# A transformer block in split fp32: seven pairs of the third layer by seven products, and tokens put in order by GpSimd

## The chip, the cores and the metric

The kernel runs on one core of one Trainium2 chip. The metric is the device time of one execution in microseconds (us). Before the change the median of three runs is 1440.94 us (1440.66 to 1441.42).

## The reference

One encoder block on x (512 tokens, width 1024, float32): a half-step SwiGLU feed-forward (the first layer here), a mixer of dilated attention and a gated recurrence (the second), and another half-step feed-forward (the third).

```python
def rmsnorm(x, g):
    return x * lax.rsqrt(jnp.mean(x * x, axis=-1, keepdims=True) + EPS) * g

def swiglu(x, w_in, w_out):
    gate, up = jnp.split(x @ w_in, 2, axis=-1)
    return (jax.nn.silu(gate) * up) @ w_out

h = rmsnorm(x, ffn1_pre_norm);  x = x + 0.5 * rmsnorm(swiglu(h, w_ffn1_in, w_ffn1_out), ffn1_post_norm)
h = rmsnorm(x, mix_pre_norm)
z = h @ w_in            # q, k, v of 3 head groups (dilations 1, 4, 16), 5 HGRN parts, 2 gates
y = (sigmoid(gA) * (attention @ P_A) + sigmoid(gH) * (hgrn2 @ P_H)) @ w_out
x = x + rmsnorm(y, mix_post_norm)
h = rmsnorm(x, ffn2_pre_norm);  x = x + 0.5 * rmsnorm(swiglu(h, w_ffn2_in, w_ffn2_out), ffn2_post_norm)
```

w_ffn2_in is 1024 x 5632 and w_ffn2_out 2816 x 1024.

## The kernel before

Activations lie transposed: 128 features to a tile, 512 tokens along the row; xt holds x in 8 such tiles (KT). Every large product is made in three passes of TensorE in a rounded fp32 format (F32R): a factor is split into a high part (rounded) and a low part (the rest), and high x high, high x low and low x high are summed in PSUM (product, project). hh and hl are the high and low parts of the normalised tokens, whi and wlo those of a weight block.

Weights come in blocks of 128x1024 floats. SyncE loads a block into raw (load_block); ScalarE copies it to whi (head), VectorE subtracts to get wlo (tail), TensorE multiplies (project). head(pair, s) and tail(pair, s) prepare the next pair's block. The counters are raw_in, head_done, split_done and block_done. Each engine runs its own list in the order in which the code writes it; only counters tie the lists together.

First half of a feed-forward: 22 pairs, each a gate block (s = 0) and an up block (s = 1) for 128 of the 2816 columns. VectorE scales each result by rstd (gated, up), ScalarE takes Silu (gate), VectorE multiplies (glu) into a_raw, which is split into ah and al for the second half.

In the first layer pairs 6 to 21 are done as Strassen products. The two column blocks, two halves of the features and two halves of the tokens give a 2x2 block product, done in 7 instead of 8 quarter products of 256 tokens (strassen_in_pe, with the order Q_ORDER and banks BANKS). VectorE forms the weight sums c and d, ScalarE and VectorE split a, b, c and d into high and low (a_part, b_part, c_part, d_part, sum_part), and results are seeded and joined through PSUM (seed_c11, u2_out, u4_out, c22_joined, c21_joined). The tokens are normalised beforehand with a negative gain (normed), and their sums formed and split once (token_sums_early and _late, b_tail, t_tail).

In the third layer (ffn3_in_pe, ffn_in_act, ffn_in_dve) all 22 pairs are direct: 0 and 1 by token halves, pair 2 into banks 5 and 6, the others in turn into banks 0 and 1 (ffn_in_turn, ffn_in_loop). After pairs 4 and 5 TensorE transposes x (turn_x, 4 tiles each time), ScalarE copies it to x_tok (leave_x) and GpSimd stores it to DRAM, from where the last stage takes it back. The second half of the layer uses Strassen sums over pairs of a_raw tiles from pair 6 on; six of its eight sets are formed during the first half (pair_sums, pair_head, pair_low), one after every two pairs.

In the mixer the values of the three head groups come first (v_pe). There the tokens are the stationary operand (128 tokens to an output bank) and the weights move. Group 0 takes tokens in order, in two halves, each tile as soon as VectorE has it (counter pre2 "ready"; VectorE's chain for a tile ends in the operation on line 1557). Groups 1 and 2 take the tokens by their remainder modulo 4, for the dilations: every fourth column of hh and hl is read as the stationary operand (line 2098). Between groups 1 and 2 the tokens are normalised anew into hh and hl (h_norm, h_head, h_low). GpSimd stores a table of bias vectors and loads the bias tiles of the head pairs; in the recurrence it copies one tile a head.

Of the kernel before, what the change touches and what calls it, by code (L numbers as in the profile page):

```python
# [19 lines left out]
ALU = mybir.AluOpType  # L20
ACT = mybir.ActivationFunctionType
AXIS_X = mybir.AxisListType.X
F32 = mybir.dt.float32
# [12 lines left out]
R = 4  # L36
# [41 lines left out]
AFTER_IH_S_SUM, AFTER_IH_T_SUM = IN_S_SUM + 8, IN_T_SUM + 4  # L78
IH_0 = 2 * FIRST["ih"]
# [38 lines left out]
def build(nc, wstream, x_t, params, last_gain, rel_bias, onehot, consts, out):  # L118
    with ExitStack() as ctx:
# [44 lines left out]
        ones = ones_r[:].bitcast(F32)  # L164
        cst = place("cst", [P, 2 * P + 2 * S])
# [80 lines left out]

        at[0] = arena + 4 * S * (2 * FT + 1)
# [112 lines left out]

        at[0] = arena
# [615 lines left out]
        def ffn3_in_pe(pe):  # L977
# [30 lines left out]
            ffn_in_turn(pe, 3, 4)  # L1008
# [15 lines left out]
        def pair_sums(dve, m):  # L1024
# [4 lines left out]
            if m < 2:  # L1029
                dve.wait_ge(sem("x_turned"), KT)  # L1030
            elif m < AHEAD_KP:
                dve.wait_ge(sem("pool_stored"), 16 * (1 + TT))
            else:
                dve.wait_ge(block_done, LAST)
# [40 lines left out]
        def ffn_in_loop(pe, n, j0):  # L1075
            with pe.Fori(j0, FT) as j:
                ffn_in_turn(pe, n, j)

        def ffn_in_act(act, n):
            first = FIRST[f"ffn{n}_in"]  # L1080

            def gate(j):
                act.wait_ge(sem("gated"), GATED_BEFORE[n] + j + 1)
                act.wait_ge(sem("glu"), BEFORE[n] + j + 1)
                nc.scalar.activation(silu[:], tmp[:, 0, :], ACT.Silu).then_inc(sem("silu"), 1)

            def pair(m):
                j = N_PLAIN + 2 * m
                for k in (j, j + 1):
                    turn(k, False)  # L1090
                if m < AHEAD_KP:
                    pair_head(act, m)

            def a_head(j):
                act.wait_ge(sem("glu"), BEFORE[n] + j + 2)
                nc.scalar.activation(ah[:, bass.ds(j, 1), :].rearrange("p a n -> p (a n)"), tmp[:, 1, :],
                                     ACT.Copy).then_inc(sem("a_head"), 1)

            def turn(j, whole=True):
                head(act, first + j, 0)  # L1100
                gate(j)
                head(act, first + j, 1)
                if whole:
                    a_head(j)
# [6 lines left out]
            a_head(0)  # L1111
            gate(1)
            head(act, first + 2, 1)
            a_head(1)
            gate(2)
            a_head(2)
            for j in range(3, 5):
                turn(j)
            leave_x(act, 0)
            turn(5)  # L1120
            leave_x(act, 1)
            for m in range(N_KP):
                pair(m)
# [2433 lines left out]
```

## Time and profile before

| what | value |
|---|---|
| median of 3 runs | 1440.94 us |
| profiled execution | 1441.15 us, span 1439.0 us, mean granted clock 0.999 |
| busy TensorE matmul / weight loads | 1431.7 / 1227.9 us |
| busy VectorE / ScalarE / GpSimd | 903.7 / 669.4 / 23.3 us |
| values, groups 1 and 2 | from 377 to 424 us |
| third layer, pairs 7 to 21 of the first half | from about 1161 us |

In the profile PE is TensorE's matmuls, PEld its weight loads, DVE VectorE, ACT ScalarE, POOL GpSimd, SP SyncE. Matmuls are pipelined: the next starts before one ends, so what one costs is read from the distance of starts and not from its length. An output is written ps<-b,w with the moving operand and the stationary one. ps is PSUM.

### The profile page before, as it was taken

The numbers are of one execution on the slowest core, as the hardware profiler recorded it, in microseconds if no ns is written. First come the engines' busy times: TensorE is split into PE (matmuls) and PEld (weight loads), VectorE is DVE, ScalarE is ACT, GpSimd is POOL, SyncE is SP. The second block draws the span as 40 slices with busy tenths as digits, with TensorE's granted clock in tenths as the row PEclk, the third lists the DMA queues.
The fourth block names the chain that finished last, engine by engine and source line by source line (L and its number), as shares of the span: only waits on it lengthen the run. The fifth ranks groups of instructions, "written<-read, shape, count | busy, mean of one in ns | idle before, by whom it ended". The sixth has DMA issues, their size and how long they took to land.

```text
span 1439.0 us, 21208 instructions
## 1 busy us (share of the span) xinstructions
PE 1431.7 (99%) x8104; PEld 1227.9 (85%) x8104; DVE 903.7 (63%) x1424; ACT 669.4 (47%) x1083; POOL 23.3 (2%) x43
## 2 busy tenths in 40 slices
PE   9999999999999999999999999999999999999998
PEld 8899999888898888888888888888889888888886
DVE  7888875335753455567866766664548555564975
ACT  5455555334532546555446554553445333233542
POOL 0000000000100000000000000000000000000000
PEclk9999999999999999999999999999999999999999
DMA  5333223324333323225322122224331243324653
GB/s 198 118 118 114 93 89 118 132 90 130 96 110 89 92 74 89 63 74 169 115 97 74 59 87 63 69 72 129 106 103 45 88 148 101 97 92 143 218 182 130
DMA packets 44317, 153.71 MB, mean 107 GB/s; under 512 B 5287, under 2 KB 5287, under 8 KB 44240
## 3 DMA queue, kind: packets, MB, share of 16 engines
q1 hardware_dynamic: 41472, 143.67, 31.3%
q0 software_dynamic: 2624, 8.95, 2.0%
q8 instruction: 51, 0.84, 0.2%
q14 instruction: 26, 0.21, 0.0%
q10 hardware_dynamic: 144, 0.04, 0.0%
HBM read 147.63 MB, written 4.23 MB: 106 GB/s over the span
## 4 chain that ended last, share of the span: by engine, by line
PE 98%; ACT 1%; DVE 1%; issue 0%; DVEq 0%; ACTq 0%
PE ps L470 21%; PE ps L471 21%; PE ps L472 21%; PE ps L637 4%; PE ps L638 4%; PE ps L639 4%; PE ps L1701 3%; PE ps L1700 3%; PE ps L1702 3%; PE ps L2530 1%; PE ps L2100 1%; PE ps L2101 1%; PE ps L2102 1%; PE ps L2913 1%; PE ps L2510 1%; PE ps L2933 1%
## 5 line engine op out<-in xcount | busy, mean ns | idle before, releaser
L470 PE MATMUL ps<-hh,whi 128*128 128x512 f32 x960 | 379.2, 395 | 0.1
L472 PE MATMUL ps<-hh,wlo 128*128 128x512 f32 x960 | 374.0, 390 | 0.0
L471 PE MATMUL ps<-hl,whi 128*128 128x512 f32 x960 | 373.9, 389 | 0.0
L416 DVE TENSOR_TENSOR wlo<-raw,whi 128x1024 fp32r<-128x1024 f32 x172 | 210.5, 1224 | 250.4 <-ACT whi L411 250.3
L411 ACT ACTIVATE whi<-raw 128x1024 fp32r<-128x1024 f32 x172 | 181.8, 1057 | 380.9 <-PE ps L472 356.3
L470 PEld LDWEIGHTS ps<-hh,whi 128*128 128x128 f32 x960 | 180.1, 188 | 42.6 <-issue 3.2
L472 PEld LDWEIGHTS ps<-hh,wlo 128*128 128x128 f32 x960 | 180.2, 188 | 38.1
L471 PEld LDWEIGHTS ps<-hl,whi 128*128 128x128 f32 x960 | 180.3, 188 | 35.7
L470 PE MATMUL ps<-ah,whi 128*128 128x512 f32 (+1 forms) x192 | 71.5, 372 | 0.0
L472 PE MATMUL ps<-ah,wlo 128*128 128x512 f32 (+1 forms) x192 | 71.3, 371 | 0.0
L471 PE MATMUL ps<-al,whi 128*128 128x512 f32 (+1 forms) x192 | 71.3, 371 | 0.0
L1700 PE MATMUL ps<-whi,ah 128*128 128x512 f32 x112 | 43.6, 389 | 0.0
L1702 PE MATMUL ps<-whi,al 128*128 128x512 f32 x112 | 43.6, 389 | 0.0
L1701 PE MATMUL ps<-wlo,ah 128*128 128x512 f32 x112 | 43.6, 389 | 0.0
L470 PEld LDWEIGHTS ps<-ah,whi 128*128 128x128 f32 x192 | 36.2, 188 | 6.3
L471 PEld LDWEIGHTS ps<-al,whi 128*128 128x128 f32 x192 | 36.2, 188 | 6.3
L472 PEld LDWEIGHTS ps<-ah,wlo 128*128 128x128 f32 x192 | 36.2, 188 | 6.2
L1145 DVE TENSOR_TENSOR tmp<-ps,rstd 128x512 f32<-128x512 f32 x22 | 15.2, 690 | 41.7 <-PE ps L472 41.6
L1134 DVE TENSOR_TENSOR tmp<-ps,rstd 128x512 f32<-128x512 f32 x22 | 15.2, 690 | 34.5 <-PE ps L472 32.0
L2594 ACT ACTIVATE prob_t<-ps 128x512 f32<-128x512 f32 x32 | 17.4, 595 | 40.2 <-PE ps L2530 38.6
L1675 ACT ACTIVATE whi<-ring 128x1024 fp32r<-128x1024 f32 x20 | 21.1, 1062 | 27.6 <-PE ps L1702 27.6
L2586 ACT ACTIVATE prob<-prob,neg_max 128x256 f32<-128x256 f32 x64 | 31.6, 503 | 2.8 <-DVE neg_max L2702 2.5
(576 smaller groups left out, 3007.4 us busy)
## 6 DMA issues: line engine op xcount, KB each, us to landing
raw<-in_wstream SPq DMA_DIRECT2D x189, 512.0 KB, 3.5
w_raw<-in_wstream SPq DMA_DIRECT2D x32, 512.0 KB, 4.3
ring<-in_wstream SPq DMA_DIRECT2D x20, 512.0 KB, 4.3
xt<-in_x_t SPq DMA_DIRECT2D x16, 256.0 KB, 4.3
raw_early<-in_wstream SPq DMA_DIRECT2D x8, 512.0 KB, 4.4
raw_late<-in_wstream SPq DMA_DIRECT2D x4, 512.0 KB, 3.9
x_dram<-x_tok POOLq DMA_DIRECT2D x4, 512.0 KB, 4.1
x_tok<-x_dram POOLq DMA_DIRECT2D x4, 512.0 KB, 5.8
```

The lines of the kernel that those rows point to most:

```text
L411: nc.scalar.activation(whi[:, s, :], raw[:, s, :], ACT.Copy).then_inc(head_done, 1)
L416: nc.vector.tensor_tensor(wlo[:, s, :], raw[:, s, :], whi[:, s, :].bitcast(F32), ALU.subtract).then_inc(split_done, 1)
L470: nc.tensor.matmul(out, w, m, start=start, stop=False)
L471: nc.tensor.matmul(out, w, ml, start=False, stop=False)
L472: return nc.tensor.matmul(out, wl, m, start=False, stop=stop)
L637: nc.tensor.matmul(out, w, b, start=q in (1, 7) and k == 0, stop=False, skip_group_check=True)
L638: nc.tensor.matmul(out, w, b_l, start=False, stop=False, skip_group_check=True)
L639: last = nc.tensor.matmul(out, wl, b, start=False, stop=k == KT // 2 - 1, skip_group_check=True)
L1700: nc.tensor.matmul(out, a, w, start=start, stop=False, skip_group_check=True)
L1701: nc.tensor.matmul(out, a, wl, start=False, stop=False, skip_group_check=True)
L1702: return nc.tensor.matmul(out, a_low, w, start=False, stop=stop, skip_group_check=True)
L2586: nc.scalar.activation(prob[:, e, lay, :], prob[:, e, lay, :], ACT.Exp, bias=stat(neg_max, n, lay, e), scale=-1.0, accum_out=stat(row_sum, ...
```

## The change

Two parts.

In the third layer pairs 7 to 13 become Strassen products, with the same steps and order as in the first layer. VectorE normalises the tokens into b3_raw and forms four token sums (the first layer keeps three); ScalarE and VectorE split them to b3_high, b3_low, t3_high, t3_low. The weights of even steps lie in the place of hh and hl, so pair 14 reads b3_high and b3_low, and during it the tokens are copied back to hh and hl (h_back). From pair 14 on the results need no scaling by rstd: ScalarE takes Silu straight from PSUM (gate_plain) and VectorE multiplies straight from PSUM (glu_plain). ah and al of tiles 0 to 5 are made three at a time in pairs 14 and 15, and the six early sets for the second half in pairs 14 to 20. turn_x(0) comes ahead of pair 4 and turn_x(1) ahead of pair 5; x goes to x_early, in two halves, each stored by itself. Pairs 5 and 6 use banks 2, 3 and 0, 1.

In the values GpSimd copies hh and hl of each tile into hp_high and hp_low with the tokens ordered by remainder, groups 1 and 2 read these, the new tokens of group 2 are written in that order, and GpSimd copies them back to hh and hl before attention. Two counters of the constant tables become one.

```diff
@@ ffn3_in_pe @@
-            ffn_in_turn(pe, 3, 4)
             pe.wait_ge(sem("gated"), GATED_BEFORE[3] + 3)
             pe.wait_ge(sem("up"), GATED_BEFORE[3] + 3)
             turn_x(pe, 0)
-            ffn_in_turn(pe, 3, 5)
+            ffn_in_turn(pe, 3, 4)
             pe.wait_ge(sem("x_left"), 4)
             turn_x(pe, 1)
-            ffn_in_loop(pe, 3, 6)
+            pe.wait_ge(sem("gated"), GATED_BEFORE[3] + 2)
+            project(pe, first + 5, 0, ps[:, 2, :], hh, hl)
...
+            strassen3_pe(pe)
+            for j in range(J4, FT):
+                early = j == J4
+                pe.wait_ge(sem("silu"), BEFORE[3] + (j if early else j + 1))
+                if j == J4 + 1:
+                    pe.wait_ge(sem("h_high"), S3_H + KT + 4)
+                    pe.wait_ge(sem("h_low"), S3_H + KT + 4)
+                h, h_l = (b3_high, b3_low) if early else (hh, hl)
+                project(pe, first + j, 0, ps[:, 0, :], h, h_l)
...
+        Q3_ORDER = []
+        for _j in range(J3, J4):
+            Q3_ORDER += [(1, _j), (7, _j)]
+            if _j > J3:
+                Q3_ORDER.append((3, _j - 1))
+            Q3_ORDER.append((6, _j))
+            if _j > J3:
+                Q3_ORDER.append((4, _j - 1))
+            Q3_ORDER += [(2, _j), (5, _j)] if _j < J4 - 1 else [(5, _j), (2, _j)]
+        Q3_ORDER += [(3, J4 - 1), (4, J4 - 1)]
...
@@ VectorE, pair 14 on @@
+            for j in range(J4, FT):
+                tail(dve, first + j, 0)
+                if j < J4 + 2:
+                    a_lows(3 * (j - J4), 3 * (j - J4) + 3)
+                if j > J4 and j - J4 - 1 < AHEAD_KP:
+                    for part in range(2):
+                        pair_low(dve, j - J4 - 1, part)
+                glu_plain(j)
+                if j - J4 < AHEAD_KP:
+                    pair_sums(dve, j - J4)
+                tail(dve, first + j, 1)
...
@@ v_pe @@
-                        if t == 0 and g == 2:
-                            pe.wait_ge(sem("h_low"), IN_H + kt + 1)
+                        if t == 0:
+                            pe.wait_ge(*((sem("h_turned"), KT + kt + 1) if g == 1 else (sem("h_low"), IN_H + kt + 1)))
...
-                        m = [x[:, kt, :].rearrange("p (u r) -> p r u", r=R)[:, t, :] for x in (hh, hl)]
+                        m = hp_high[kt][:, t, :], hp_low[kt][:, t, :]
...
@@ gpsimd @@
+            for kt in range(KT):
+                pool.wait_ge(*counted("pre2", "ready", KT + kt + 1))
+                nc.gpsimd.tensor_copy(hp_high[kt][:], hh[:, kt, :].rearrange(by_rest, r=R)).then_inc(sem("h_turned"), 1)
+            pool.wait_ge(block_done, 2 * FIRST["v"] + 2)
+            for kt in range(KT):
+                nc.gpsimd.tensor_copy(hp_low[kt][:], hl[:, kt, :].rearrange(by_rest, r=R)).then_inc(sem("h_turned"), 1)
             pool.wait_ge(sem("vec_out"), 2)
...
+                        pool.wait_ge(sem("h_turned"), 2 * KT)
+                        for d in range(KT):
+                            pool.wait_ge(sem("h_low"), IN_H + d + 1)
+                            for x, turned in ((hh, hp_high[d]), (hl, hp_low[d])):
+                                nc.gpsimd.tensor_copy(x[:, d, :].rearrange(by_rest, r=R), turned[:]
+                                                      ).then_inc(sem("h_turned"), 1)
```

GpSimd's list from the constant tables to the bias tiles, before; vec_dram is the table of bias vectors.

```order
L3299 DMA hot_sb<-in_onehot 33x1024
L3300 DMA cst<-in_consts 128x1280
L3302 DMA vec_dram<-vec_sb 8x1024 [waits vec_out]
L3320 DMA bias_156<-vec_dram 128x384 [waits post_x,pool_stored]
L3321 DMA bias_156<-vec_dram 128x2x128
...
L3311 DMA v_mid<-v_tok 64x1536 [waits v_scaled]
```

The same place after; the lines with "..." between them are seven more copies of the same kind each time.

```order
L3737 DMA cst<-in_consts 128x1280
L3740 COPY hp_high_242<-hh 128x512 [waits pre_ready]
...
L3743 COPY hp_low_250<-hl 128x512 [waits block_done]
...
L3745 DMA vec_dram<-vec_sb 8x1024 [waits vec_out]
L3768 DMA bias_179<-vec_dram 128x384 [waits post_x,pool_stored]
L3769 DMA bias_179<-vec_dram 128x2x128
...
L3756 COPY hh<-hp_high_242 128x4x128 [waits h_low,h_turned]
L3756 COPY hl<-hp_low_250 128x4x128
...
L3759 DMA v_mid<-v_tok 64x1536 [waits v_scaled]
```

Sixteen copies stand ahead of the bias table's DMA, and sixteen ahead of v_mid's.

VectorE's list in the third layer for one direct pair and the sums behind it, before (a pair's gate, up and product, the weights' low parts between them).

```order
L1134 TENSOR_TENSOR tmp<-ps,rstd 128x512 [waits silu,block_done]
L416 TENSOR_TENSOR wlo<-raw,whi 128x1024 [waits head_done]
L1145 TENSOR_TENSOR tmp<-ps,rstd 128x512 [waits glu,block_done]
L416 TENSOR_TENSOR wlo<-raw,whi 128x1024 [waits head_done]
L1150 TENSOR_TENSOR a_raw<-silu,tmp 128x512 [waits up,silu]
L1036 TENSOR_TENSOR t_raw_a<-a_raw 128x256 [waits glu,x_turned]
```

One Strassen step of the third layer after, from one join to the next.

```order
L1546 TENSOR_TENSOR tmp<-ps,tmp 128x256 [waits glu,q_left]
L1506 TENSOR_TENSOR w_even_c_raw<-w_raw 128x1024 [waits block_done,raw_in1,raw_in0]
L1534 TENSOR_TENSOR w_even_a_low<-w_raw,w_even_a_high 128x1024 [waits head_done]
L1524 TENSOR_TENSOR w_even_d_raw<-w_even_c_raw,w_raw 128x512 [waits s_sum]
L1514 TENSOR_TENSOR w_even_c_low<-w_even_c_raw,w_even_c_high 128x1024 [waits s_sum,s_head]
L1528 TENSOR_TENSOR w_even_d_raw<-w_even_d_raw,w_raw 128x512 [waits s_sum]
L1551 TENSOR_TENSOR tmp<-ps,y_67 128x256 [waits block_done]
L1435 TENSOR_TENSOR a_raw<-silu,tmp 128x512 [waits q_joined,silu]
L1514 TENSOR_TENSOR w_even_d_low<-w_even_d_raw,w_even_d_high 128x1024 [waits s_sum,s_head]
L1540 TENSOR_TENSOR w_even_b_low<-w_raw,w_even_b_high 128x512 [waits head_done]
```

A pair's five operations become ten, in which the scaling by rstd no longer occurs.

## Rows read from the trace of the kernel before

**Rows 1.** The page, busy time and chain that ended last.

```profile
PE 1431.7 (99%) x8104; PEld 1227.9 (85%) x8104; DVE 903.7 (63%) x1424; ACT 669.4 (47%) x1083; POOL 23.3 (2%) x43
...
PE 98%; ACT 1%; DVE 1%; issue 0%; DVEq 0%; ACTq 0%
```

**Rows 2.** Waits of TensorE (us in total, times, longest).

```profile
PE ps L3343 <- DVE eps L3394: 1.7, 1, 1.7
```

**Rows 3.** Timeline (start, length us) and one stretch by engine, first and third layer.

```profile
99.75 0.28 PE L637 MATMUL ps<-b_high,w_even_a_high 128*128 128x256 f32 x1
...
199.68 0.28 PE L637 MATMUL ps<-b_high,w_even_a_high 128*128 128x256 f32 x1
...
99.75:199.68 99.93, 99.93 (x843) 99.93 (x841) 80.65 (x101) 53.28 (x80) 0.00 (x0) 1.00 0.31 106
...
1157.34 0.39 PE L470 MATMUL ps<-hh,whi 128*128 128x512 f32 x1
...
1195.42 0.39 PE L470 MATMUL ps<-hh,whi 128*128 128x512 f32 x1
```

**Rows 4.** The page's costliest groups, VectorE.

```profile
L416 DVE TENSOR_TENSOR wlo<-raw,whi 128x1024 fp32r<-128x1024 f32 x172 | 210.5, 1224 | 250.4 <-ACT whi L411 250.3
...
L1145 DVE TENSOR_TENSOR tmp<-ps,rstd 128x512 f32<-128x512 f32 x22 | 15.2, 690 | 41.7 <-PE ps L472 41.6
```

**Rows 5.** Timeline of TensorE, first Strassen pair of the first layer.

```profile
77.97 0.28 PE L639 MATMUL ps<-b_high,w_first_a_low 128*128 128x256 f32 x1
78.23 0.38 PE L637 MATMUL ps<-b_high,w_first_c_high 128*128 128x256 f32 x1
78.45 0.28 PE L638 MATMUL ps<-b_low,w_first_c_high 128*128 128x256 f32 x1
```

**Rows 6.** Timeline of TensorE, third layer, ahead of pair 4.

```profile
1124.60 0.39 PE L472 MATMUL ps<-hh,wlo 128*128 128x512 f32 x1
1125.12 0.47 PE L470 MATMUL ps<-hh,whi 128*128 128x512 f32 x1
1125.43 0.40 PE L471 MATMUL ps<-hl,whi 128*128 128x512 f32 x1
```

**Rows 7.** Two lines (ns min/median/max) and TensorE's timeline, values' last groups.

```profile
L2100 PEld LDWEIGHTS ps<-whi,hh x64: 307/309/314, 376.9 to 423.2; 128*128 128x128 f32 x64
...
L2278 PEld LDWEIGHTS ps<-whi,hl x24: 187/188/188, 676.0 to 713.4; 128*128 128x128 f32 x24
...
376.93 0.63 PE L2100 MATMUL ps<-whi,hh 128*128 128x512 f32 x1
...
394.78 0.91 PE L2115 MATMUL ps<-cst,rstd 32*128 32x32 f32 x8
395.62 0.62 PE L2100 MATMUL ps<-whi,hh 128*128 128x512 f32 x1
...
424.12 0.40 PE L470 MATMUL ps<-hh,whi 128*128 128x512 f32 x1
```

**Rows 8.** Timeline of VectorE and TensorE, values' first group.

```profile
363.74 0.48 DVE L1557 SCALAR_TENSOR_TENSOR hl<-xt,par,hh 128x256 fp32r<-128x256 f32 x1
...
364.76 0.40 PE L2079 MATMUL ps<-whi_v,hh 128*128 128x512 f32 x1
...
371.68 0.48 DVE L1557 SCALAR_TENSOR_TENSOR hl<-xt,par,hh 128x256 fp32r<-128x256 f32 x1 [0.18 <-ACT hh L1463]
...
375.58 0.39 PE L2081 MATMUL ps<-wlo_u,hh 128*128 128x512 f32 x1
```

**Rows 9.** GpSimd's copy (a line, the timeline) and the last new tokens' split.

```profile
L3327 POOL COPY y<-ih_tok x8: 606/615/616, 721.1 to 934.2; 128x512 f32 x8
...
721.15 0.61 POOL L3327 COPY y<-ih_tok 128x512 f32 x1 [180.02 <-DVE ih_tok L2358]
...
721.47 0.48 DVE L3034 MEMSET rstd<- 128x512 f32 x1
...
405.43 1.35 DVE L2186 TENSOR_TENSOR hl<-tmp,hh 128x512 fp32r<-128x512 f32 x2
```

More of the change, by code:

```diff
@@ new lines, in glu_plain, with a_lows @@
+            def glu_plain(j):
+                dve.wait_ge(block_done, 2 * (first + j) + 2)
+                dve.wait_ge(sem("silu"), BEFORE[3] + j + 2)
+                if j == J4:
+                    dve.wait_ge(sem("h_low"), S3_H + KT + 4)
+                nc.vector.scalar_tensor_tensor(out=a_raw[:, j, :], in0=ps[:, 1, :], scalar=-1.0, in1=silu[:], op0=ALU.mult,
+                                               op1=ALU.mult).then_inc(sem("glu"), 1)
+            def a_lows(j0, j1):
+                flat = "p k n -> p (k n)"
+                dve.wait_ge(sem("a_head"), BEFORE[3] + j1)
+                high, low, whole = [x[:, j0:j1, :].rearrange(flat) for x in (ah, al, a_raw)]
+                nc.vector.tensor_tensor(low, whole, high.bitcast(F32), ALU.subtract).then_inc(sem("a_tail"), j1 - j0)
@@ L1191, in ffn_in_dve @@
             tail(dve, first + 2, 0)
[L1192 removed]
+            glu_whole(0)
             gated(1, 2)
             up(1, 3)
[L1195 to L1196 removed]
+            normed(0)
+            glu_whole(1)
             gated(2, 5)
             up(2, 6)
[L1199 to L1203 removed]
+            tail(dve, first + 2, 1)
+            glu_whole(2)
@@ new lines, in ffn3_in_dve @@
+            for kt in (4, 1, 5):
+                normed(kt)
+            gated(3, 0)
+            tail(dve, first + 3, 0)
+            for kt in (2, 6, 3, 7):
+                normed(kt)
+            up(3, 1)
+            tail(dve, first + 3, 1)
+            glu_whole(3)
+            token_sums_early()
+            gated(4, 0)
+            tail(dve, first + 4, 0)
+            token_sums_late()
+            b_tail(0)
+            up(4, 1)
+            tail(dve, first + 4, 1)
+            glu_whole(4)
@@ new lines, in ffn3_in_dve @@
+            b_tail(1)
+            for k in range(KT // 2):
+                t_tail(k)
+            gated(5, 2)
+            tail(dve, first + 5, 0)
+            b_tail(2)
+            b_tail(3)
+            c_sum(J3)
+            tail(dve, first + 5, 1)
+            up(5, 3)
+            glu_whole(5)
+            gated(6, 0)
+            a_part(J3)
+            d_sums(J3)
+            up(6, 1)
+            glu_whole(6)
+            for j in range(J3, J4):
+                nxt = j + 1
+                sum_part(j, "d")
+                b_part(j)
+                if j > J3:
+                    c22_joined(j - 1)
+                if nxt < J4:
+                    c_sum(nxt)
+                    a_part(nxt)
+                    d_sums(nxt)
+                else:
+                    tail(dve, first + J4 - 1, 0)
+                if j > J3:
+                    c21_joined(j - 1)
+                    glu_whole(j - 1)
```

516 lines of the change are left out of this document (412 added, 104 removed).

## The prediction

> **What bounds the kernel now.** I read the page first: its busy line and its chain of waits. The busy line gives TensorE 1431.7 us of a span of 1439.0 us, VectorE 903.7, ScalarE 669.4 and GpSimd 23.3; the chain that ended last is 98% TensorE [rows 1]. Then the waits of TensorE: a single one, 1.7 us, at the program's start [rows 2]. So TensorE is never kept waiting long, and only two things can save time: fewer or faster matmuls, or the removal of small gaps. Work on another engine is free as long as it isn't late. The question for every edit is therefore what it does to TensorE's list, and whether a step that feeds TensorE becomes late. TensorE's rows are pipelined, so a row's own duration (390 ns, 283 ns) is not what it costs; the distance between two starts is. I use the timeline for that.
>
> **Seven pairs of the third layer by seven products.** A pair (a gate block and an up block of 128 columns) is now 2 blocks x 8 token tiles x 3 passes = 48 matmuls of 512 columns. In an undisturbed stretch of the third layer 168 of them lie between starts 1157.34 and 1195.42, 38.08 us: 0.2267 us each, 10.88 us a pair [rows 3]. A Strassen pair is 7 products x 4 tiles x 3 passes = 84 matmuls of 256 columns. The first layer already runs sixteen: the same matmul of pairs ten apart starts at 99.75 and at 199.68, so 9.99 us a pair, with every seed, sum and join hidden [rows 3]. Each pair saves 10.88 - 9.99 = 0.89 us, seven save 6.2 us.
>
> What must be ready: every loop step gives VectorE and ScalarE the same operations as in the first layer, and the first layer shows that they fit. Only the way in and the way out differ. On the way in VectorE has, between the rstd and the end of the seventh direct pair, 31 operations 512 wide (gate, up and product of seven pairs, eight normalised tiles, two weight sums) and 23 that are 1024 wide (splits and sums): at 0.69 and 1.22 us [rows 4] 21.4 + 28.1 = 49.5 us, less where they overlap. There are about 51 us for them: eight blocks of 5.44 us, two sets of transposes, and some 4 us before the first block. I laid the list out in order against TensorE's blocks. TensorE waits nowhere; the closest is the low part of the weights of pair 6's gate, made about 1.5 us before it is wanted, behind four splits of the token sums. The copies of x out to DRAM go earlier, to two places of their own, and end some 8 us before their space is written. At the change from plain to Strassen pairs the first layer loses little: starts 77.97, 78.23, 78.45 instead of 0.12 us apart, 0.24 us [rows 5]. I take 0.3 us here.
>
> One gap goes. In the third layer TensorE stands from 1124.60 to 1125.12 and is slow to 1125.43, 0.38 us above two plain steps, since the low part for pair 4 comes late [rows 6]. The transposes of x are now put in front of that pair and cover it: -0.4 us. On the way out, copying the tokens back (four copies on each of ScalarE and VectorE, at most 1.2 us each) lies beside pair 14's 10.9 us. In pairs 14 to 20 the sums for the second product come at one set a pair instead of one in two; the fullest pair has about 10.4 us on VectorE, 0.4 us before TensorE wants its last split. I cost that at nothing; if it slips, it is some tenths a pair. Third layer: -6.2 + 0.3 - 0.4 = -6.3 us.
>
> **The values' last two groups.** Their stationary operand is read with a stride of four elements: its load takes 309 ns, where a load of the same shape with tokens in order, in a later stage, takes 188 ns [rows 7]. From 376.93 to 424.12 are 47.19 us; 0.84 us are the transposes (394.78 to 395.62), the rest, 46.35 us, 192 matmuls and two for a sum [rows 7]. At 0.2267 us they would take 43.98 us, so at most 2.4 us can be won. Of this about 0.8 us is at starts after a break, where a load stands open, and only part of that goes. Lower bound: the first group, which reads its tokens in order, runs from 364.76 to 375.58 with 47 steps [rows 8], 0.230 us; if the group's pace has another cause than the stride, little is won, some 0.3 us. I take 2.0 us, since the load's row is plainly the thing that differs.
>
> **What GpSimd's copies cost.** They are the unknown. Eight copies (128x512) put the high tokens in order, each as soon as a tile's second half is ready; eight for the low tokens follow when the first group is done; sixteen bring the new tokens back later. The nearest row is a copy of the same size, tokens not strided, 615 ns [rows 9]. If they disturb nobody, the last high copy ends about 0.6 us after the last tile, and the first low copy at 375.58 + 0.39 + 0.62 = 376.6, before TensorE's 376.93: no cost.
>
> But while the high copies run, VectorE is what feeds TensorE. Its last operation for a tile (L1557) ends at 364.22 for the second half of tile 0 and at 372.16 for tile 7: 1.13 us a tile [rows 8]. TensorE takes 1.38 us a tile from 364.76 on and wants tile 7 at 374.5, so there are 2.3 us to spare. If a copy of length c holds VectorE up for its whole length, each tile becomes later by c, and TensorE stands 7c - 2.3 us. The trace has no copy beside a VectorE operation that reads two tensors. The copy at 721.15 runs beside a memset at its usual 0.48 us [rows 9], which reads nothing: the lower bound is no effect. With c = 0.61 the stall is 2.0 us, plus some 0.3 us for the first low copy. I take this middle value, one whole copy handed over per tile, because nearly all VectorE operations there read two SBUF tensors and so does nothing in that row. The copies back can start only as the new tiles come, the last at about 406.8 (405.43 plus 1.35) [rows 9], with 17 us left before attention asks for them at 424 [rows 7]; two copies of up to 0.6 us each for a tile fit: nothing. The vector table's DMA and the bias DMAs queue behind GpSimd's copies, some us later than now, and are wanted only in attention.
>
> The Trainium skill ("SBUF — State Buffer", two separate sides) says that GpSimd and a VectorE operation with two SBUF inputs exclude each other for the whole instruction. By that rule the 2.3 us are paid; no row of before shows it. The skill's "GPSIMD Engine Reference" (pitfalls) says that reads with a step above 8 bytes cost about half as much again, 2.9 instead of 1.9 cycles an element. By that the copy would be an estimated 0.93 us, the stall 4.2 us, and the time about 1437; no row here shows that either.
>
> **The sum.** -6.3 - 2.0 + 2.3 = -6.0 us. The profiled execution took 1441.15 us (span 1439.0), 0.2 us above the median of the runs, 1440.94; I take the difference from the median: 1434.9, say 1435.0 us.
>
> **Rivals.** First, the copies disturb nobody: -8.3 us, 1432.6. For it: the memset beside the copy is unchanged. Against: a memset needs no read. Second, the third layer slips: VectorE, busy 80.65 of 99.93 us in a Strassen stretch [rows 3] and fuller on the way in, is late in each pair, say 0.6 us, and half of the gain goes with it; with the copies' cost, 1438 to 1439. Against it: the first layer's ten pairs at exactly 9.99 us. Third, and on the other side: the strided copies are long and VectorE waits for each. The stall is 7c - 2.3 and the first low copy adds c - 0.6, so the whole gain of 8.3 us is gone at c of about 1.4 us, and at c = 1.8 us, three times the row, the kernel stands near 1444, slower by 0.2%. For it: the reads are strided, which no row prices for GpSimd. Against it: the factor of three; TensorE's own strided load is only 309/188 = 1.6 times as long.
>
> **How the numbers follow.** Copies held up moderately, my forecast: 0.45 (1434 to 1437.5). No disturbance: 0.33 (1432 to 1433.5). The third layer slips: 0.09 (1437 to 1440). Long copies, over 0.9 us held up: 0.13 (1437 to 1445). Range 1431.8 to 1439.5. A difference of 0.2%, 2.9 us, is about what a measurement of this kernel can tell from none. Faster by more (below 1438.1): nearly all of the first two and some of the others, 0.85. Within it: 0.10. Slower: 0.05.
>
> **What would show it.** Seven pairs of 9.99 us in the third layer, with no row of TensorE waiting for VectorE or ScalarE there beyond tenths; no gap before pair 4; loads of 188 ns and starts 0.227 us apart in the values' last two groups. For the copies: their duration; the distance between the L1557 operations of neighbouring tiles (1.13 us if undisturbed, about 1.75 if I am right); and a wait of TensorE of about 2 us between 365 and 377. I am wrong if that wait is absent (then 1432.6), if it is over 4 us, or if a Strassen pair of the third layer takes more than 10.1 us.

## The result, and the profile after

The changed kernel takes 1452.67 us (median of 6 runs, 1450.75 to 1454.39), the kernel before 1441.24 us in the same runs. The ratio is 1.0079, with a 95% interval of 1.0067 to 1.0092: slower by 11.4 us, where I had forecast 6 us faster. In the profile the span grows from 1439.0 to 1451.1 us. Two landmarks split it. Attention's first matmul starts at 441.89 instead of 424.12, so the values are 17.8 us later. The first matmul of the third layer's second half moves from 1324.62 to 1336.70, 12.1 us later, so the third layer won 5.7 us. The values are where the forecast failed: I had them at -2.0 + 2.3 = +0.3 us, and they cost 17.8.

The page after, busy time and the chain that ended last (beside [rows 1]):

```profile
PE 1430.4 (99%) x8356; PEld 1227.7 (85%) x8356; DVE 961.3 (66%) x1464; ACT 698.3 (48%) x1126; POOL 71.8 (5%) x75
...
PE 95%; DVE 3%; issue 1%; ACT 1%; DMA 0%; SPq 0%; DVEq 0%; ACTq 0%
```

TensorE's busy time fell by 1.3 us only, and that hides both gain and loss: around its longer waits the clock was lowered, and each matmul then counts longer. The chain tells more: VectorE holds 3% of it instead of 1. TensorE's waits after (us in total, times, longest; beside the one row of [rows 2]; one more of 0.3 us lies in the first layer):

```profile
PE ps L2529 <- ACT v_tok L2550: 6.8, 1, 6.8
PE ps L2529 <- DVE v_tok L2606: 3.1, 1, 3.1
PE ps L2508 <- DVE hl L1986: 1.7, 5, 0.4
PE ps L3793 <- DVE eps L3845: 1.7, 1, 1.7
PE ps L2529 <- issue: 1.5, 1, 1.5
```

L2508 is the values' group 0, L2529 groups 1 and 2; only the row of L3793 was there before. Now VectorE beside GpSimd in group 0 (timeline: start, length; L1986 hands a tile's second half to TensorE, beside [rows 8]):

```profile
363.84 0.48 DVE L1986 SCALAR_TENSOR_TENSOR hl<-xt,par,hh 128x256 fp32r<-128x256 f32 x1
364.23 0.42 DVE L1967 TENSOR_TENSOR tmp<-gained_y,rstd 128x256 f32<-128x256 f32 x1
364.69 1.23 DVE L1980 TENSOR_TENSOR xt<-xt,tmp 128x256 f32<-128x256 f32 x1
365.84 0.47 DVE L1986 SCALAR_TENSOR_TENSOR hl<-xt,par,hh 128x256 fp32r<-128x256 f32 x1
...
367.80 0.47 DVE L1986 SCALAR_TENSOR_TENSOR hl<-xt,par,hh 128x256 fp32r<-128x256 f32 x1
...
364.38 1.25 POOL L3740 CAST hp_high<-hh 128x512 fp32r<-128x512 f32 x1 [350.27 <-DVE hl L1986]
```

The same operation of VectorE before, where its line is L1551:

```profile
364.59 0.43 DVE L1551 TENSOR_TENSOR xt<-xt,tmp 128x256 f32<-128x256 f32 x1
```

Read them against each other. The copy begins at 364.38 while VectorE's L1967 runs, which keeps its 0.42 us. The next operation, L1980, starts at 364.69 and ends at 365.92, 0.29 us after the copy's end at 365.63. Before it took 0.43 us. So it is held for 0.8 us, nearly until the copy ends. A tile now comes every 1.98 us on average (363.84, 365.84, 367.80) and TensorE wants one every 1.38.

TensorE's timeline in groups 1 and 2 after (beside [rows 7]), and then two stretches by engine (busy time of TensorE, its loads, VectorE, ScalarE and GpSimd, the granted clock, DMA share and GB/s):

```profile
380.23 0.28 PE L548 MATMUL ps<-hot_r,table_l 33*8 33x256 f32 x1
381.99 0.47 PE L2529 MATMUL ps<-whi,hp_high 128*128 128x512 f32 x1 [1.48 <-issue]
...
386.72 0.50 PE L2529 MATMUL ps<-whi,hp_high 128*128 128x512 f32 x1 [3.11 <-DVE v_tok L2606]
...
417.64 0.77 PE L2529 MATMUL ps<-whi,hp_high 128*128 128x512 f32 x1 [6.81 <-ACT v_tok L2550]
```

```profile
417.60:421.60 4.00, 3.96 (x9) 3.14 (x10) 4.00 (x5) 0.85 (x1) 4.00 (x4) 0.50 0.00 0
387.50:391.00 3.50, 3.50 (x10) 2.74 (x9) 3.29 (x3) 1.26 (x2) 3.50 (x3) 0.55 0.02 5
```

For the wait of 1.48 us the profile names no releaser; by the code it is for the first low copy, and without the copies ahead it is gone. The other two are 3.11 us for VectorE's copy of group 0's result out of PSUM, 6.81 us for ScalarE's of group 1. Behind each of these two the granted clock is about half, 1.2 instead of 2.4 GHz, and matmuls start 0.43 instead of 0.23 us apart: some 1.5 us lost up to 391.1, 1.9 us up to 421.6. The ledger of the values: 3.5 (the bias matmuls behind group 0, 375.90 to 379.41) + 1.5 + 3.1 + 1.5 + 6.8 + 1.9 = 18.3 us, less some 0.7 us of faster matmuls, so 17.6 against 17.8 seen.

Why ScalarE's copy came late stands in VectorE's list ahead of group 2, since ScalarE's next operations follow VectorE's. L2611 normalises the new tokens with strided reads:

```profile
400.68 2.19 DVE L2611 SCALAR_TENSOR_TENSOR tmp<-xt,par,rstd 128x512 f32<-128x512 f32 x2
402.77 1.49 DVE L2618 TENSOR_TENSOR hp_low<-tmp,hp_high 128x512 fp32r<-128x512 f32 x2
404.19 3.61 DVE L2611 SCALAR_TENSOR_TENSOR tmp<-xt,par,rstd 128x512 f32<-128x512 f32 x2
407.71 2.78 DVE L2618 TENSOR_TENSOR hp_low<-tmp,hp_high 128x512 fp32r<-128x512 f32 x2
```

The copies back, one line's summary (ns: minimum, median, maximum; first and last start):

```profile
L3756 POOL CAST hh<-hp_high x8: 1099/1755/2103, 403.6 to 427.1; 128x512 fp32r<-128x512 f32 x8
```

The first pair runs with GpSimd idle, the second beside the copies back, which begin at 403.6: 2.19 becomes 3.61 and 1.49 becomes 2.78 us. Where I took 0.6 us, a copy back takes 1.76.

In the third layer the same matmul of steps four apart:

```profile
1196.35 0.28 PE L1182 MATMUL ps<-b_high,w_even_a_high 128*128 128x256 f32 x1
...
1236.67 0.28 PE L1182 MATMUL ps<-b_high,w_even_a_high 128*128 128x256 f32 x1
```

That is 10.08 us a pair, no wait, where the first layer takes 9.99 [rows 3]. The gap ahead of pair 4 [rows 6] is gone.

### The profile page after: what moved, and what is told of

It reads as the page before. It is cut to its first block, busy times and chain, and to the rows that moved or that the text cites. A ratio compares the mean times of both kernels' runs of the same rounds, so it can differ in the third digit from the quotient of the medians.

```text
span 1451.1 us, 21760 instructions
## 1 busy us (share of the span) xinstructions
PE 1430.4 (99%) x8356; PEld 1227.7 (85%) x8356; DVE 961.3 (66%) x1464; ACT 698.3 (48%) x1126; POOL 71.8 (5%) x75
## 4 chain that ended last, share of the span: by engine, by line
PE 95%; DVE 3%; issue 1%; ACT 1%; DMA 0%; SPq 0%; DVEq 0%; ACTq 0%
PE ps L524 20%; PE ps L526 19%; PE ps L525 19%; PE ps L691 4%; PE ps L692 4%; PE ps L693 4%; PE ps L2131 3%; PE ps L2130 2%; PE ps L2129 2%; PE ps L1182 2%; PE ps L1183 2%; PE ps L1184 2%; PE ps L2963 1%; PE ps L3346 1%; PE ps L2943 1%; PE ps L3366 1%
## 5 line engine op out<-in xcount | busy, mean ns | idle before, releaser
L470 DVE TENSOR_TENSOR wlo<-raw,whi 128x1024 fp32r<-128x1024 f32 x158 | 195.7, 1239 | 257.1 <-ACT whi L465 257.0
L524 PE MATMUL ps<-hh,whi 128*128 128x512 f32 x832 | 329.3, 396 | 0.0
L526 PE MATMUL ps<-hh,wlo 128*128 128x512 f32 x832 | 324.2, 390 | 0.0
L525 PE MATMUL ps<-hl,whi 128*128 128x512 f32 x832 | 324.0, 389 | 0.0
L465 ACT ACTIVATE whi<-raw 128x1024 fp32r<-128x1024 f32 x158 | 167.0, 1057 | 297.5 <-PE ps L526 274.9
L524 PEld LDWEIGHTS ps<-hh,whi 128*128 128x128 f32 x832 | 156.1, 188 | 36.9 <-issue 2.6
L526 PEld LDWEIGHTS ps<-hh,wlo 128*128 128x128 f32 x832 | 156.2, 188 | 33.2
L525 PEld LDWEIGHTS ps<-hl,whi 128*128 128x128 f32 x832 | 156.3, 188 | 30.8
L2529 PE MATMUL ps<-whi,hp_high 128*128 128x512 f32 x64 | 27.2, 424 | 11.4 <-ACT v_tok L2550 6.8
L3027 ACT ACTIVATE prob_t<-ps 128x512 f32<-128x512 f32 x32 | 17.4, 595 | 40.2 <-PE ps L2963 38.6
L3135 DVE CUSTOM_DVE_ANT_0 prob<-ps,bias 128x256 f32<-128x256 f32 x64 | 23.3, 420 | 14.0 <-PE ps L2930 14.0
```

The costliest lines, as they stand in the source:

```text
L465: nc.scalar.activation(whi[:, s, :], raw[:, s, :], ACT.Copy).then_inc(head_done, 1)
L470: nc.vector.tensor_tensor(wlo[:, s, :], raw[:, s, :], whi[:, s, :].bitcast(F32), ALU.subtract).then_inc(split_done, 1)
L524: nc.tensor.matmul(out, w, m, start=start, stop=False)
L525: nc.tensor.matmul(out, w, ml, start=False, stop=False)
L526: return nc.tensor.matmul(out, wl, m, start=False, stop=stop)
```

## The experiments

Twelve kernels ran, in four batches, each beside the kernel before, which took 1441.2 to 1441.4 us throughout. Their line numbers differ a little from the changed kernel's.

### One part alone

```diff
@@ e1_layer3_only: groups 1 and 2 as before, GpSimd's copies gone @@
-                        m = hp_high[kt][:, t, :], hp_low[kt][:, t, :]
+                        m = [x[:, kt, :].rearrange("p (u r) -> p r u", r=R)[:, t, :] for x in (hh, hl)]
@@ e2_values_only: the kernel before with the values as changed @@
```

> The changed kernel without its part in the values (tokens read with the stride again, no copies by GpSimd); the third layer as changed. Theory A: all of the 11.4 us lost and more come from the values (+17.7 us there in the trace), and the third layer gives 5.6 us, so about 1435.6. Rival B: the third layer's gain is bought elsewhere too, or the two parts disturb each other, and the time is above 1438.

> The kernel before with only the part in the values (copies by GpSimd in both directions). Theory A: 1441.2 + 17.7 = about 1459. Rival B (the parts disturb each other): under 1454.

The third layer alone: 1435.28 us (1434.85 to 1435.53), ratio 0.9955 (0.9939 to 0.9972), 6.1 us faster. The values alone: 1458.56 us (1457.04 to 1460.45), ratio 1.0114 (1.0097 to 1.0131), 17.2 us slower. The two add up to -6.1 + 17.2 = 11.1 us, within 0.3 of the whole, so neither part disturbs the other. The first is also the best version found that computes everything; it beats both kernels.

### Copies taken away, ahead or back

```diff
@@ e3_no_copies_back @@
-                            for x, turned in ((hh, hp_high[d]), (hl, hp_low[d])):
-                                nc.gpsimd.tensor_copy(x[:, d, :].rearrange(by_rest, r=R), turned[:]
...
@@ e4_no_copies_ahead: group 1 reads hh and hl with stride @@
-                nc.gpsimd.tensor_copy(hp_high[kt][:], hh[:, kt, :].rearrange(by_rest, r=R)).then_inc(sem("h_turned"), 1)
-                nc.gpsimd.tensor_copy(hp_low[kt][:], hl[:, kt, :].rearrange(by_rest, r=R)).then_inc(sem("h_turned"), 1)
```

> The changed kernel without GpSimd's sixteen copies back to hh and hl (attention then reads the tokens of the first group, so that part computes with other numbers). Theory A (a copy holds up VectorE's operations with two inputs in SBUF, and TensorE waits for what VectorE makes): the 6.8 us wait before group 2 shrinks to 1 to 2 us, no fall of the clock behind it, about 1445. VectorE's normalisation still takes about 1.1 us each, since it reads with a stride. Rival B (the strided normalisation alone makes the wait, the copies back hold nothing): the wait stays above 5 us, over 1450.

> The changed kernel without the sixteen copies ahead of group 1, which reads hh and hl with the stride as before; group 2 and the copies back as changed. Theory A: group 0 runs as before the change (no 3.5 us), TensorE doesn't wait for the first low copy (1.5 us) nor for VectorE's v_tok (3.1 us and the slow clock behind it), about 1444. Rival B (the delay in group 0 has another cause): the 3.5 us stay, over 1447.

Without the copies back: 1447.99 us (1446.78 to 1448.24), ratio 1.0041 (1.0027 to 1.0055), 3 us over theory A's figure and 2 under B's. The wait ahead of group 2 shrank from 6.8 to 2.3 us but did not go; something else held VectorE there. Without the copies ahead: 1444.63 us (1443.72 to 1445.17), ratio 1.0021 (1.0012 to 1.0031), as A expected. Group 0 is undisturbed and a wait of 6.6 us for ScalarE's copy is left. The two savings, 4.7 and 8.0 us, don't exhaust the 17.4 us between the changed kernel and the third layer alone, so a third piece remained, or the two overlap.

### Neither copies nor a strided normalisation

```diff
@@ e6_no_copies_at_all: both edits above @@
@@ e7_no_copies_norm_in_order: and then @@
-                nc.vector.scalar_tensor_tensor(out=tmp[:, d % 2, :].rearrange("p (r u) -> p r u", r=R),
-                                               in0=xt[:, d, :].rearrange(by_rest, r=R), scalar=PRE2[:, d:d + 1],
-                                               in1=rstd[:].rearrange(by_rest, r=R), op0=ALU.mult, op1=ALU.mult
...
+                nc.vector.scalar_tensor_tensor(out=tmp[:, d % 2, :], in0=xt[:, d, :], scalar=PRE2[:, d:d + 1],
+                                               in1=rstd[:], op0=ALU.mult, op1=ALU.mult).then_inc(sem("h_norm"), 1)
```

> The changed kernel without any of GpSimd's copies, ahead of group 1 or back: group 1 reads hh and hl with stride as before, group 2 reads the tokens written in order of remainder. Attention then reads the first normalisation's tokens (left out: the copying back). The normalisation still reads x and rstd with stride. Theory A (GpSimd's copies did the damage, the strided read costs VectorE 0.38 us a tile and no more): the chain of new tokens takes 16.6 - 2 = about 14 us instead of 16.6, so the wait ahead of group 2 is 1 to 3 us, without the copies 1436 (1435 to 1437). Theory B (group 2's strided normalisation alone makes most of the wait of 6.6 us seen without the copies ahead): 1440 or more, with the wait still over 5 us.

> The same, and the new tokens are normalised and read in token order (left out: the order by remainder in group 2). No operation of VectorE reads with stride. Both theories: no wait ahead of group 2 beyond that of the kernel before; group 1 reads with stride, group 2 in order, so of the 2.0 us that I put on both groups' stationary operand 1.0 comes: 1435.3 (third layer alone) - 1.0 = 1434.3. If the stationary operand's stride costs nothing in time, 1435.3 again.

The first: 1437.56 us (1436.74 to 1439.65), with a wait of 2.1 us ahead of group 2, 0.6 us over A's range; theory B, which wanted over 5, falls. With both kinds of copy gone 15.1 us are saved, more than 4.7 + 8.0, so the savings don't simply add. The second: 1435.00 us (1434.60 to 1435.09), no wait. So the strided read alone costs 2.6 us. It takes 0.40 us more for each of eight tiles (0.75 to 1.15 us), and six of them, 2.4 us, come before ScalarE's copy out of PSUM, for which TensorE waits 2.1 us: a chain with 0.3 us of slack. That is the third piece.

The second run misses its own figure of 1434.3. Group 2 reads its stationary operand in order there and group 1 with stride, and the kernel is only 0.3 us below the third layer alone, which reads both with stride (their runs overlap, and each against its own kernel before they are 0.1 us apart). So the times don't resolve this gain, but the trace does. Two stretches of that run, first in group 1, then in group 2, and the loads of each:

```profile
380.01:393.87 13.86, 13.86 (x60) 13.78 (x60) 7.06 (x9) 5.84 (x8) 5.08 (x8) 1.00 0.59 164
402.54:420.81 18.27, 18.27 (x80) 14.94 (x79) 10.72 (x16) 5.44 (x7) 1.06 (x2) 1.00 0.46 130
```

```profile
L2530 PEld LDWEIGHTS ps<-whi,hh x32: 307/309/311, 377.1 to 400.7; 128*128 128x128 f32 x32
...
L2530 PEld LDWEIGHTS ps<-whi,hp_high x32: 187/188/188, 401.5 to 422.9; 128*128 128x128 f32 x32
```

Between starts lie 13.86 / 59 = 0.235 us with stride and 18.27 / 79 = 0.2313 in order, 0.35 us over a group's 96 matmuls. Nearly all of a load of 309 or 188 ns lies beside the matmul before it. Where TensorE starts after a break it is exposed: the second matmul of group 1 comes 0.47 us after the first with stride (before) and 0.30 in order (after). Even in order the distance is 0.2313 and not the third layer's 0.2267 us; why is open.

### Single operations, alone and together

> Leaves out the whole computation: it runs series of single operations on 128x512 tiles, first each engine alone (GpSimd: copy rounded to F32R in order; read with stride 4; the same two as plain F32; written with stride 4. VectorE: difference of two tiles; product of two tiles; the same product read with stride 4; copy out of PSUM; copy within SBUF; product of PSUM and a tile. ScalarE: copy in order and read with stride 4), then VectorE's series beside GpSimd's strided copies, VectorE's beside GpSimd's copies in order, ScalarE's beside GpSimd's strided copies. Theory A (the stride makes GpSimd's copy long, and a VectorE operation with two operands in SBUF and a GpSimd copy take turns): GpSimd in order about 0.61 us in both formats, with stride 1.2; VectorE 0.7 alone and 1.4 to 1.8 beside strided copies for the two-operand operations, but unchanged for the copy out of PSUM and the product with PSUM; GpSimd's copies 1.5 to 2 us beside them; beside copies in order VectorE loses about half as much. Theory B (the rounding makes GpSimd's copy long): 1.2 us in order too when rounded, 0.6 with stride in plain F32. Theory C (GpSimd slows every VectorE operation, through the banks of SBUF): the copy out of PSUM, which also writes SBUF, and the copy within SBUF grow by the same share. ScalarE by A and B is unchanged beside GpSimd and its strided read costs nothing extra (0.65 us); by C it grows.

```diff
@@ e5_operations_alone_and_together: the whole kernel is this @@
+        pool_read = lambda i: g.tensor_copy(p_r[:, i, :].rearrange(in_rest, r=R), a[:, i, :].rearrange(by_rest, r=R))
+        pool_flat = lambda i: g.tensor_copy(p_r[:, i, :], a[:, i, :])
+        tt = lambda i: v.tensor_tensor(v_r[:, i, :], b[:, i, :], c[:, i, :], ALU.subtract)
+        leave = lambda i: v.tensor_copy(v_f[:, i, :], ps[:, i, :])
...
```

It ran once. GpSimd alone (L55 in order; L54 with stride, L56 the same without rounding; L58 written with stride), VectorE alone (L60, L61 in order, L63 with stride), ScalarE alone (L70 in order); then VectorE beside strided copies, one row of it beside copies in order (105.46), and ScalarE with stride beside strided copies:

```profile
11.68 2.28 POOL L55 CAST p_r<-a 128x512 fp32r<-128x512 f32 x4 [11.23 <-SPq L86]
14.02 4.16 POOL L54 CAST p_r<-a 128x512 fp32r<-128x512 f32 x4
20.59 4.16 POOL L56 COPY p_f<-a 128x512 f32<-128x512 f32 x4
24.81 3.91 POOL L58 CAST p_r<-a 128x512 fp32r<-128x512 f32 x4
28.79 2.50 DVE L60 TENSOR_TENSOR v_r<-b,c 128x512 fp32r<-128x512 f32 x4 [14.89 <-SPq L94]
31.33 2.74 DVE L61 SCALAR_TENSOR_TENSOR v_f<-b,par,c 128x512 f32<-128x512 f32 x4
34.10 4.22 DVE L63 SCALAR_TENSOR_TENSOR v_f<-b,par,c 128x512 f32<-128x512 f32 x4
...
40.87 1.43 DVE L67 COPY v_f<-b 128x512 f32<-128x512 f32 x4
42.34 2.48 DVE L68 TENSOR_TENSOR v_f<-ps,c 128x512 f32<-128x512 f32 x4
44.89 2.19 ACT L70 ACTIVATE s_r<-b 128x512 fp32r<-128x512 f32 x4 [42.88 <-SPq L94]
...
51.27 5.17 DVE L60 TENSOR_TENSOR v_r<-b,c 128x512 fp32r<-128x512 f32 x4 [6.45 <-SPq L94]
62.44 7.45 DVE L63 SCALAR_TENSOR_TENSOR v_f<-b,par,c 128x512 f32<-128x512 f32 x4
69.92 2.48 DVE L66 COPY v_f<-ps 128x512 f32<-128x512 f32 x4
72.44 4.55 DVE L67 COPY v_f<-b 128x512 f32<-128x512 f32 x4
77.03 2.48 DVE L68 TENSOR_TENSOR v_f<-ps,c 128x512 f32<-128x512 f32 x4
...
105.46 3.73 DVE L60 TENSOR_TENSOR v_r<-b,c 128x512 fp32r<-128x512 f32 x4 [25.94 <-SPq L94]
...
141.04 4.11 ACT L71 ACTIVATE s_r<-b 128x512 fp32r<-128x512 f32 x4
```

Two of these stretches by engine (busy time and operations of VectorE, ScalarE and GpSimd), VectorE's differences of two SBUF tiles and its copies out of PSUM:

```profile
51.30:56.44 5.14, 5.14 (x4) 0.00 (x0) 5.14 (x4) 1.00 0.00 0
69.92:72.40 2.48, 2.48 (x4) 0.00 (x0) 2.42 (x3) 1.00 0.00 0
```

Each row of the timeline is four operations, so a quarter of it is one:

| 128x512, us each | alone | beside strided copies | beside copies in order |
|---|---|---|---|
| VectorE difference of two SBUF tiles (L60) | 0.63 | 1.29 | 0.93 |
| VectorE product read with stride (L63; in order 0.69) | 1.06 | 1.86 | 1.39 |
| VectorE copy within SBUF (L67) | 0.36 | 1.14 | 0.70 |
| VectorE copy out of PSUM, PSUM times a tile (L66, L68) | 0.62 | 0.62 | 0.62 |
| GpSimd copy, in order / with stride | 0.57 / 1.04 | | |
| ScalarE copy, in order / with stride | 0.55 / 1.03 | 0.56 / 1.03 | |

Theory B falls: rounding costs GpSimd nothing, the stride makes the copy 1.8 times as long. Theory C falls: operations with an operand in PSUM don't notice GpSimd at all. Theory A holds in kind. In the first stretch four operations and four copies take 5.14 us, one to one, while beside the PSUM operations GpSimd copies just as busily and VectorE loses nothing. Its sizes were off (1.04 for 1.2 us, 1.29 for 1.4 or more), and it has two misses. A one-operand copy within SBUF is held up too, and ScalarE's strided read isn't free: 1.03 for 0.55 us. A copy written with stride, as the copies back are, takes 0.98 us alone. The Trainium skill ("SBUF — State Buffer", two separate sides) states an exclusive lock for the whole instruction, for two-input operations and for VectorE's two-port modes such as an fp32 copy within SBUF; by that rule both the held-up copy and the untouched PSUM operations are what one expects, and this run agrees. On the length it agrees less: an operation and a copy in full turns would take 0.63 + 1.04 = 1.67 us, and they took 1.29.

### Copies ahead: how long, how many, where

```diff
@@ e10_gpsimd_copies_in_order, against e11_gpsimd_copies_strided @@
-                nc.gpsimd.tensor_copy(hp_high[kt][:], hh[:, kt, :].rearrange(by_rest, r=R)).then_inc(sem("h_turned"), 1)
+                nc.gpsimd.tensor_copy(hp_high[kt][:].rearrange("p r u -> p (r u)"), hh[:, kt, :]).then_inc(sem("h_turned"), 1)
...
@@ e12_gpsimd_copies_after_feed @@
+            pool.wait_ge(*counted("pre2", "ready", 2 * KT))
+            for part in ("H0", "H1", "H2", "L0", "L1", "H3", "L2", "L3", "H4", "L4", "H5", "L5", "H6", "L6", "H7", "L7"):
...
```

> Third layer as changed; GpSimd copies the tokens ahead of group 1 at the same places as in the changed kernel, but each in token order, so that nothing is read with stride (left out: the order of tokens in the last two groups, and the copies back; the new tokens are normalised in order too). Its base without any copies took 1435.0. Theory A (a copy takes a share of VectorE's time in proportion to its length; by the changed kernel a copy of 1.24 us made each tile 1.98 - 1.13 = 0.85 us later, 0.7 of its length): copies of 0.6 to 0.7 us, a tile every 1.6 us, group 0 ends 7 x 0.45 - 2.3 = 0.9 us later than undisturbed (375.9), the kernel near 1436.3 (1435.5 to 1437.5). By my prediction's own rule (a whole copy per tile): 2.0 us later, 1437.3. Theory B (what counts is the number of handovers, not the length): as late as with strided copies, +3.5 us in group 0 and 1440 or more.

> The same with the strided copies of the changed kernel ahead of group 1 (left out: the copies back, and the order in which the new tokens are normalised). It differs from the run before in the copies' stride alone, and from the run without copies back in VectorE's strided normalisation alone. Theory A: group 0 ends at about 379.4, 3.5 us late; the low copies delay the next group's weights and the copies out of PSUM; the whole 1448.0 less 2.3 (the wait ahead of group 2, which I put on the strided normalisation) = about 1445 (1444 to 1446). Theory C (the wait ahead of group 2 in the run without copies back came from the late start and not from the strided normalisation): 1447.5 to 1448.

> The same strided copies, but none begins before VectorE has handed over the last tile of group 0; then high and low parts alternate so that each tile is in order before TensorE wants it (left out as in the two runs before). Theory A (the harm is done where VectorE feeds TensorE directly): group 0 ends undisturbed at 375.9; 16 copies of 1.1 to 1.5 us lie beside the sums of squares, at 2.8 us a tile TensorE needs two copies (2.2 to 3.0 us), so it is hardly kept waiting by them, but the copy out of PSUM in group 1 comes 1 to 3 us late behind the sums: 1437 to 1439. Theory D (wherever the copies lie, VectorE is the engine behind the values, and time is only moved): 1443 or more.

In order: 1438.50 us (1437.59 to 1440.15), 3.5 over the kernel without copies (1435.00); with stride 1444.59 (1443.37 to 1445.83), 9.6 over it; after the feed 1440.85 (1440.52 to 1441.67), 5.9 over it. Group 0 in the run in order:

```profile
365.18 0.72 DVE L1980 TENSOR_TENSOR xt<-xt,tmp 128x256 f32<-128x256 f32 x1
365.82 0.47 DVE L1986 SCALAR_TENSOR_TENSOR hl<-xt,par,hh 128x256 fp32r<-128x256 f32 x1
...
364.87 0.74 POOL L3738 CAST hp_high<-hh 128x512 fp32r<-128x512 f32 x1 [350.70 <-DVE hl L1986]
```

The next tile's L1986 starts at 367.30: a tile every 1.48 us, against 1.19 undisturbed (in the run of the third layer alone the L1986 operations start at 364.14, 365.33 and 366.52) and 1.98 with stride. The delay a tile is 0.29 us for a copy that alone takes 0.57 and 0.79 for one of 1.04: the copy's length less about 0.27, presumably what still runs on VectorE when the copy begins (two lengths only, so no rule). In group 0 length counts, as A had it and B had not, but at its end A had put the whole cost, and the time lies 1.0 us over A's range: group 0's bias matmuls come only 0.35 us later (at 376.84, with tile 0's L1986 at 364.33, against 376.30 and 364.14 in the run of the third layer alone), and most of the loss is a wait of 2.7 us for the copy out of PSUM, with slow matmuls behind it. (The profiled execution, 1440.15, was the slowest of the ten.) The run with stride hit A's 1445 and refuted C: with and without the strided normalisation, 1447.99 and 1444.59, it costs 3.4 us beside the late group. The run after the feed lies between A's and D's figures. Group 0 ended undisturbed, and the cost moved on. VectorE there:

```profile
373.04 3.25 DVE L470 TENSOR_TENSOR wlo<-raw,whi 128x1024 fp32r<-128x1024 f32 x2
376.22 1.57 DVE L2407 TENSOR_TENSOR y<-sq 128x512 f32<-128x512 f32 x1
...
373.19 5.57 POOL L3743 CAST hp_high<-hh 128x512 fp32r<-128x512 f32 x3 [358.99 <-DVE hl L1986]
```

Three copies take 5.57 us beside the weights' low parts (3.25 us for two, undisturbed 2.35), TensorE waits 2.4 us for the first tile and 0.9 us for ScalarE's copy out of PSUM, its clock is at half from 380 to 386, and a sum of 0.7 us takes 1.5.

### Copies by ScalarE

```diff
@@ e8_scalare_copies_group1, ScalarE's list @@
+                    nc.scalar.activation(y[:], x[:, d, :].bitcast(F32).rearrange(by_rest, r=R), ACT.Copy
+                                         ).then_inc(sem("h_turned"), 1)
...
+            turned("H0", "H1", "H2", "H3")
             square_act(act, "pre2", 0)
...
@@ e9_scalare_copies_both: the same behind h_head and h_low, and group 2 reads hp_high, hp_low @@
```

> The third layer as changed; in the values ScalarE instead of GpSimd copies the tokens for group 1 into order, high parts in its idle time ahead of the squares and low parts after group 0; group 2 reads with stride as before. Full computation. Theory A (only GpSimd disturbs VectorE; ScalarE's copies are 0.65 us each and fit in its idle time): VectorE's operations keep their length, group 1 gains 1.0 less about 0.4 at its start: 1434.7 (1434.2 to 1435.3). Theory C (any engine's strided copies slow VectorE): group 0 or the new tokens late, 1437 or more.

> As the run before, and ScalarE copies the new tokens for group 2 too, from hh and hl after their split (nothing to copy back, since hh and hl stay in token order). Full computation. Theory A: another 1.0 off, 1433.7, if the chain of new tokens (per two tiles now 4 copies and 2 heads of ScalarE, 3.9 us) does not fall behind TensorE, which takes 2.8 us a tile; at most 1 us of it lost at the start of group 2: 1433.7 to 1434.7. By the rival (ScalarE becomes the bound of the chain, and the wait ahead of group 2 is 2 us or more) 1436.

Both miss: 1440.43 us (1439.58 to 1441.79), ratio 0.9996 (0.9987 to 1.0006), and 1450.48 us (1449.99 to 1451.82), 5.2 and 15.2 over the third layer alone. VectorE keeps its lengths, so C is no cause. ScalarE's copies do the harm by themselves, in the run for group 1:

```profile
371.40 4.17 ACT L2573 ACTIVATE hp_high<-hh 128x512 fp32r<-128x512 f32 x4
...
376.65 0.69 DVE L2407 TENSOR_TENSOR y<-sq 128x512 f32<-128x512 f32 x1 [2.37 <-ACT sq L2414]
...
380.60 1.28 DVE L2628 COPY v_tok<-ps 128x512 f32<-128x512 f32 x2
```

I had priced a copy at 0.65 us; with stride it is 1.04. The squares start late, VectorE's sums wait for them, and the copy out of PSUM behind those starts at 380.60 instead of 377.52: TensorE waits 2.6 us there, and 1.3 and 0.8 us more at two other places. For group 2 as well, ScalarE becomes the bound, as the rival had it, but the wait is 10.1 us and not some 2.

## Why the prediction was wrong, step by step

**Third layer, -6.3 us: right.** Measured alone -6.1 us, by the landmarks -5.7. The terms were 0.89 a pair (seen 10.88 - 10.08 = 0.80, so -5.6 instead of -6.2; a small miss), +0.3 at the entry (starts 1184.49, 1184.74, 1184.96: as taken), -0.4 for the gap (gone). No operation was late. Why the matmuls of the third layer start 0.120 us apart and those of the first 0.119 is open; it was not tried.

**Values, -2.0 us: mis-sized.** I divided the stretch by an ideal pace and gave the stride the difference. A group's 96 matmuls gain 0.35 us, both groups 0.7. The load's row (309 against 188 ns) was plain but mostly beside other work. My lower bound, from group 0's pace, was nearer to the truth than the value I took: in order the pace is 0.2313 us, so more than half of the difference from the ideal 0.2267 has another cause than the stride.

**GpSimd's copies, +2.3 us: the step that failed.** The copies, with the strided normalisation that came with them, cost 18.5 us (17.8 seen and 0.7 gained), in three places. First, the smaller part, the length: I took 0.61 us, the row of a copy in order, and it is 1.04 alone and 1.24 beside VectorE. My rule, 7c - 2.3, had the right form: with the 0.79 us by which a tile really came later it gives 3.2 us, where 3.5 were seen and 2.0 forecast. The Trainium skill's rule in "GPSIMD Engine Reference" (performance pitfalls), half as much again for steps over 8 bytes, pointed the right way and was too small: 1.04 / 0.57 is 1.8.

Second, the larger part, the copies that I priced at nothing or 0.3 us. The low copies held up VectorE's sums, and behind them stood a copy out of PSUM for which TensorE waits. The copies back did the same to the new tokens. I looked for slack only at their consumer, attention, 17 us away; what they disturb is VectorE's list beside them.

Third, the strided normalisation, which the prediction doesn't price at all. I had taken its diff for a change of addresses. It costs 0.40 us a tile on VectorE, and the kernel 2.6 us without the copies ahead and 3.4 with them.

The runs close the sum, each row one edit further:

| kernel | us | step |
|---|---|---|
| third layer alone | 1435.3 | |
| group 2 reads in order, no copies | 1435.0 | -0.3 |
| + strided copies ahead of group 1, which reads them | 1444.6 | +9.6 |
| + strided normalisation | 1448.0 | +3.4 |
| + copies back (the changed kernel) | 1452.7 | +4.7 |

In another order the steps differ: the copies ahead cost 8.0 us where the copies back are there, and 10.4 where only the strided normalisation is.

**The rivals.** The third, long copies that VectorE waits for, came nearest, and I gave it 0.13. But it failed at the same step. A tile was held up by 0.79 us, less than the 0.9 that it named, and its range, to 1445, ended 7.7 us short. By its own rule copies of 1.24 us cost 7 x 1.24 - 2.3 + 0.6 = 7.0 us, which gives 1439.6; the argument against it, that a copy three times the row is unlikely, was even right, for it was twice the row. It counted only the high copies and the first low one, and with 1.24 us the copies ahead already cost 9.6 us. What I overlooked in all cases is what follows a wait: the clock at half for 3 to 4 us, 1.5 and 1.9 us more.

## What to carry to other kernels

Before moving a strided copy to an idle engine, price the stride on that engine and then look at what else the operation holds up: GpSimd's copy cost little on GpSimd and 9.6 us on VectorE's list. An operation whose access pattern changes in a diff is a changed operation and gets its own term. And a load that is longer by 120 ns, beside a matmul, is worth what the distance of starts shows, here 4 ns each, and more only at a start after a break.

## What was unexpected in the hardware

Reading fp32 with a step of 16 bytes slowed every engine that did it: VectorE's product 0.69 to 1.06 us, ScalarE's copy 0.55 to 1.03, GpSimd's 0.57 to 1.04, TensorE's stationary load 188 to 309 ns. The Trainium skill ("SBUF — State Buffer", in the section on the port swizzle) tells of lines of 16 bytes, with full bandwidth only when a line is used at least twice; a step of 16 bytes uses each once, and all four rows agree with that. The same passage names a step of 4 fp32 as free, and against that stand all four. No other step was measured, so the line as the cause is not shown. ScalarE was slowed by its own stride and not by GpSimd's strided copies (0.56 and 1.03 us beside them, 0.55 and 1.03 alone), and VectorE was untouched where one operand lay in PSUM (0.62 us).
